# One hybrid pooling and attention layer on one core: unnormalised transposes, interleaved first tiles, tanh gates, and an output that is filled with x first and added to by DMA

## The reference

```
hn    = rmsnorm(concat(meta, x)) * norm_g              # 1040 x 2048
pv, pg, q, k, v, ag = split(hn @ w_in)                 # 1024,1024,1024,128,128,1024 columns
pool  = (trailing mean of pv over 2/4/8/16 frames - pv) @ pool_w[group] * pool_scale
attn  = softmax([q_n k_n^T / 8, sink]) v               # 16 q heads, 2 kv heads, head size 64;
                                                       # own and previous chunk of 64, meta always
mixed = concat(silu(pg) * pool, silu(ag) * attn)
out   = x + mixed @ w_out                              # meta rows dropped
```

## Time and profile before

| | |
|---|---|
| median of three executions | 1256.48 us |
| the profiled execution's own time | 1255.78 us |
| its span in the trace | 1254.1 us |
| PE busy | 1232.8 us (98%) |
| DVE busy | 896.8 us (72%) |
| ACT busy | 635.2 us (51%) |
| DMA | 134.38 MB, 107 GB/s over the span |

### The profile page before, as it was taken

One profiled execution on the slowest core, in us unless ns is written; L12 is line 12 of the kernel. 1 busy time (PEld: TensorE's weight loads), 2 busy tenths in 40 slices (PEclk: granted clock), 3 DMA queues, 4 the chain that ended last, 5 costly groups with the idle time before them and its releaser, 6 DMA issues.

```text
span 1254.1 us, 19307 instructions
## 1 busy us (share of the span) xinstructions
PE 1232.8 (98%) x6200; PEld 1041.8 (83%) x6200; DVE 896.8 (72%) x1425; ACT 635.2 (51%) x1490; POOL 67.8 (5%) x78
## 2 busy tenths in 40 slices
PE   4999999999999999999999999999999999999998
PEld 4988898898988978888888888888888888788887
DVE  7557786888879886565654677788798887854553
ACT  6434456465563655544533345655646557444442
POOL 0000000010020110000000000000101102000000
PEclk9999999999999999999999999999999999999999
DMA  5232333222332225544533332233322232333442
GB/s 217 80 93 78 97 95 85 84 73 71 102 89 76 79 67 201 185 134 160 192 120 91 92 102 85 85 84 86 99 76 85 76 99 86 116 127 128 165 142 84
DMA packets 70609, 134.38 MB, mean 107 GB/s; under 512 B 8064, under 2 KB 10240, under 8 KB 69888
## 3 DMA queue, kind: packets, MB, share of 16 engines
q1 hardware_dynamic: 68160, 125.17, 32.2%
q0 software_dynamic: 2384, 8.39, 1.9%
HBM read 125.14 MB, written 8.39 MB: 106 GB/s over the span
## 4 chain that ended last, share of the span: by engine, by line
PE 93%; DVE 3%; ACT 1%; DMA 1%; issue 1%; SPq 0%; DVEq 0%; ACTq 0%
PE R L1072 18%; PE R L1077 18%; PE R L1073 18%; PE S L1296 4%; PE S L1297 4%; PE S L1295 4%; PE OP L1297 2%; PE OP L1295 2%; PE R L1296 2%; PE OP L1296 2%; PE R L1297 2%; PE R L1295 2%; PE OP L1073 1%; PE OP L1072 1%; PE OP L1077 1%; PE S L1196 1%
## 5 line engine op out<-in xcount | busy, mean ns | idle before, releaser
L442 ACT ACTIVATE wh<-raw 128x512 fp32r<-128x512 f32 x400 | 250.3, 631 | 488.8 <-PE R L1077 265.0
L737 DVE TENSOR_TENSOR wl<-raw,wh 128x512 fp32r<-128x512 f32 x400 | 281.1, 706 | 237.1 <-ACT wh L442 235.9
L1072 PE MATMUL R<-act_h,wh 128*128 128x512 f32 (+1 forms) x1168 | 425.1, 369 | 0.2
L1073 PE MATMUL R<-act_l,wh 128*128 128x512 f32 (+1 forms) x1168 | 419.5, 364 | 0.0
L1077 PE MATMUL R<-act_h,wl 128*128 128x512 f32 (+1 forms) x1168 | 401.5, 364 | 0.0
L1072 PEld LDWEIGHTS R<-act_h,wh 128*128 128x128 f32 x1168 | 220.0, 188 | 34.8 <-DVE wl L737 0.9
L1073 PEld LDWEIGHTS R<-act_l,wh 128*128 128x128 f32 x1168 | 220.0, 188 | 32.7
L1077 PEld LDWEIGHTS R<-act_h,wl 128*128 128x128 f32 x1168 | 210.3, 188 | 35.8
L961 DVE RECIPROCAL scr<-scr 128x512 f32<-128x512 f32 x32 | 107.3, 3353 | 1.1
L414 POOL TENSOR_TENSOR scr<-scr 128x527 f32<-128x527 f32 (+3 forms) x40 | 49.8, 1245 | 793.0 <-ACT pv_last L442 363.3
L442 ACT ACTIVATE pm<-OP 16x128 fp32r<-16x128 f32 x256 | 68.3, 267 | 5.4
(11 more groups left out here) (206 smaller groups left out, 1825.7 us busy)
## 6 DMA issues: line engine op xcount, KB each, us to landing
raw<-w_in_blocks SPq DMA_DIRECT2D x272, 256.0 KB, 2.6
raw<-w_out_in SPq DMA_DIRECT2D x128, 256.0 KB, 3.0
scr<-xcat SPq DMA_DIRECT2D x32, 256.0 KB, 4.1
mixed<-xcat SPq DMA_DIRECT2D x4, 1024.0 KB, 7.6
res<-xcat SPq DMA_DIRECT2D x16, 256.0 KB, 3.2
out<-scr POOLq DMA_DIRECT2D x14, 256.0 KB, 2.6
out<-res POOLq DMA_DIRECT2D x14, 256.0 KB, 4.5
scr<-pool_w_in SPq DMA_DIRECT2D x8, 256.0 KB, 3.2
```

What stands on the lines that cost most here:

```text
L442: return nc.scalar.activation(dst, src, ACT.Copy)
L737: return nc.vector.tensor_tensor(dst, a, b, ALU.subtract)
L1072: mm(o, wh[:, b, w], xh, start=(k == 0), stop=False)
L1073: mm(o, wh[:, b, w], xl, start=False, stop=False)
```

## The change

- **No scaling before the transposes.** The raw frames of the first half are transposed, and only the gain norm_g is applied. The 528 reciprocal roots (and EPS times the mean square) are brought into rows `rb` and `r_eps` that hold a value for each frame on all partitions: ACT spreads them in `r_columns`, PE transposes them (`r_transposes`), ACT copies them out (`r_rows`). V, the gates and the pooled values of the first half are multiplied by `rb`; q and k, which are normalised anyway, only get `r_eps` in place of EPS (`k_mean`, `q_mean`).
- **First loads and first tiles.** The frames come in five loads by channel blocks (`FIRST_LOADS`: blocks 0-1, 2-3, 4-7, 8-11, 12-15), with the first weight blocks between them. The K and V tiles are interleaved block by block (`first_tiles`). `r_columns` stands on ACT ahead of Q slot 0, `r_transposes` on PE in Q slot 1, `r_rows` on ACT in slot 2, `q_mean(t)` on DVE in slot 4t + 5. The squares of K are summed in Q slot 2 and the V windows made in Q slot 8.
- **Gates by tanh.** silu(z) = z/2 (1 + tanh(z/2)): one activation and one DVE operation; in the first half one more DVE operation for `rb`. The factor 1/2 goes into `hscale` and the attention product.
- **Output.** After the last Q block of the first half SP issues eight copies from x to `out`, each 128 rows (1 MB), DRAM to DRAM. DVE only copies a product out of PSUM; POOL's queue adds it to `out` by an accumulating DMA. The residual loads and SP's last stores are gone.
- **Places.** The four operand buffers of the output projection that lie in `band_h` and `band_x` start at other columns; other tiles move with the size of `junk`, which is now part of `row_buf`.

```diff
-            sp.dma_start(x_meta, xcat[0:META, :]).then_inc(s_xf[ROWT], 16)
-            sp.dma_start(x_first[0], xcat[META:META + P, :]).then_inc(s_xf[0], 16)
-            sp.dma_start(cst[:, :], consts).then_inc(s_cst, 16)
...
+            def first_frames(i):
+                k0, k1 = FIRST_LOADS[i]
+                lo, hi = k0 % 4 * P, (k1 - 1) % 4 * P + P
+                sp.dma_start(mixed[:, k0 // 4:KT:4, lo:hi],
+                             xcat[META:META + HALF, k0 * P:k1 * P].rearrange("(r p) c -> p r c", p=P)).then_inc(s_xf[i], 16)
+            sp.dma_start(cst[:, 0:P], consts[:, 0:P]).then_inc(s_id, 16)
+            sp.dma_start(x_meta, xcat[0:META, :]).then_inc(s_xmeta, 16)
+            first_frames(0)
+            sp.dma_start(vec[:, :], vecs).then_inc(s_vec, 16)
+            first_block(0, free=False)
+            first_frames(1)
...
                 with sp.Fori(0, PAIRS) as j:
                     for b in range(TILE_BLKS):
                         n = KV_BLKS + j * TILE_BLKS + b
                         load_block(h0 + n, b % RAW, w_in[n, :, :])
+                if h == 0:
+                    for r in range(ROWT * HALVES):
+                        sp.dma_start(out[P * r:P * (r + 1), :], xcat[META + P * r:META + P * (r + 1), :]).then_inc(s_pre, 16)
                 sp.wait_ge(s_free, ONE + h * OB * ROWT)
...
-                        if RES_LOAD <= k < RES_LOAD + ROWT:
-                            r = k - RES_LOAD
-                            sp.dma_start(y[r], xcat[h * HALF + META + P * r:h * HALF + META + P * (r + 1),
-                                                    bass.ds(nb * BLK, BLK)]).then_inc(s_res[r], 16)
...
+                pool.wait_ge(s_pre, 16 * ROWT * HALVES)
+                with pool.Fori(0, OB) as nb:
                     for r in range(ROWT):
                         pool.wait_ge(s_ye, YB_FREE + (h * OB + nb) * ROWT + r + 1)
                         pool.dma_start(out[h * HALF + P * r:h * HALF + P * (r + 1), bass.ds(nb * BLK, BLK)],
-                                       y[r]).then_inc(s_out[r], 16)
+                                       y[r], accum_op=ALU.add).then_inc(s_out[r], 16)
...
+                        if h == 0:
+                            pool.tensor_tensor(pv_last[:, g * 2 + jj, :], pv[jj][:, COLS - META:COLS],
+                                               rb[:, COLS - META:COLS], ALU.mult).then_inc(s_pvl, 1)
+                            pool.tensor_tensor(pv[jj][:, :], pv[jj][:, :], rb[:, :], ALU.mult).then_inc(s_pvr, 1)
...
-        mix_h = [band_h[:, 0, 0:BLK], band_h[:, 1, 0:BLK],
+        mix_h = [band_h[:, 0, 64:64 + BLK], band_h[:, 1, 48:48 + BLK],
-        mix_l = [band_x[:, 0, 0:BLK], band_x[:, 1, 0:BLK], mix_x[:, 0, :], mix_x[:, 1, :]]
+        mix_l = [band_x[:, 0, 160:160 + BLK], band_x[:, 1, 144:144 + BLK], mix_x[:, 0, :], mix_x[:, 1, :]]
...
+                def r_columns():
+                    act.wait_ge(s_xrs, 2)
+                    for r in range(ROWT):
+                        copy(r_col[:, r, :], xrs[:, r:r + 1].to_broadcast([P, P])).then_inc(s_rc, 1)
+                        nc.scalar.activation(e_col[:, r, :], xsd[:, r:r + 1].to_broadcast([P, P]), ACT.Square,
+                                             scale=EPS ** 0.5).then_inc(s_rc, 1)
...
+                def r_rows():
+                    act.wait_ge(s_rt, 1)
+                    copy(rb[:, META:COLS], PT[:, :]).then_inc(s_rb, 1)
+                    copy(rb[:, 0:META], PM[:, 0:META]).then_inc(s_rb, 1)
+                    copy(r_eps[:, META:COLS], S[:, 1, :]).then_inc(s_rb, 1)
...
+                def q_mean(t):
+                    dve.wait_ge(s_qss, t + 1)
+                    nc.vector.scalar_tensor_tensor(q_rs[t % 2], (PT, PM)[t % 2][:, :], 1.0 / HD, r_eps[:, META:COLS],
+                                                   ALU.mult, ALU.add).then_inc(s_qm, 1)
...
-                        nc.vector.tensor_scalar(gate[n], gate[n], 1.0, None, ALU.add).then_inc(s_ga, 1)
-                        nc.vector.reciprocal(gate[n], gate[n]).then_inc(s_gr, 1)
-                        nc.vector.tensor_tensor(gate[n], bank[:, :], gate[n], ALU.mult).then_inc(s_gt[n], 1)
+                        tanh, u = (gate_t, gate[n]) if h == 0 else (gate[n], bank[:, :])
+                        nc.vector.scalar_tensor_tensor(gate[n], tanh, 1.0, u, ALU.add, ALU.mult).then_inc(s_gt[n], 1)
...
-                    nc.vector.tensor_tensor(y[r], YB[r], y[r], ALU.add).then_inc(s_ye, 1)
+                    nc.vector.tensor_scalar(y[r], YB[r], 1.0, None, ALU.mult).then_inc(s_ye, 1)
...
+            def first_tiles(h):
+                for n in range(KV_BLKS):
+                    b, banks = n // 2, (KB, VB)[n % 2][h]
+                    pe.wait_ge(s_wl, ONE + h * NBLK + n + 1)
...
                 def q_events(s):                       # PE, after each Q block
-                    if s == 0:
+                    if s == 1 and h == 0:
+                        r_transposes()
+                    elif s == 2:
+                        k_squares()
+                    elif s == 8:
                         v_windows()
```

More of the change, by code:

```diff
@@ L273, in hymba_layer @@
         s_ge = [sem(f"s_ge{n}") for n in range(4)]
-        s_ga = sem("s_ga")
-        s_gr = sem("s_gr")
+        s_gv = [sem(f"s_gv{n}") for n in range(4)]
         s_gt = [sem(f"s_gt{n}") for n in range(4)]
@@ L451, in split_high, with stats @@
                 copy(wh[:, slot, :], raw[:, slot, :]).then_inc(s_wh, 1)
-            def stats(x, rows, squares, n, col, loaded, loads):
-                act.wait_ge(loaded, 16 * loads)
+            def stats(x, rows, squares, n, col):
                 nc.scalar.activation(junk[0:rows, :], x[0:rows, :], ACT.Square,
@@ L494, in _ @@
                                      scale=vec[:, V_G + k:V_G + k + 1]).then_inc(s_xh, 1)
-                if k in FIRST_SPLITS and FIRST_SPLITS[k] >= RAW:
-                    split_high(0, FIRST_SPLITS[k])
+                for off in FIRST_SPLITS.get(k, ()):
+                    split_high(0, off)
+            act.wait_ge(s_cst, 16)
+            for i in range(len(FIRST_LOADS)):
+                act.wait_ge(s_xf[i], 16)
+            first_stats(0)
+            first_stats(1)
+            act.wait_ge(s_init, 5)
             for h in range(HALVES):
@@ L521, in _ @@
-                product_done(act, h, TILE_BLKS)
-                for bank, c in span_banks(h, VB[h]):
-                    own_v, frames = own_part(bank, c)
-                    copy(vT[:, CHUNK + frames.start:CHUNK + frames.stop], own_v).then_inc(s_vT, 1)
-                if h == 0:
-                    copy(v_meta[:, :], R[2][:, 0:META]).then_inc(s_vT, 1)
+                    if h == 0 and s < 7:
+                        first_stats(s - 3)
+                if h == 0:
+                    act.wait_ge(s_xm, 1)
+                    root(META, ROWT)
@@ L529, in v_all_out @@
+                if h == 0:
+                    r_columns()
                 def v_all_out():
@@ L703, in _ @@
                     group(g)
[L704 removed]
+                act.wait_ge(s_qn, (h + 1) * PAIRS)
                 group(2)
@@ new lines, in k_mean, with v_out @@
+                def k_mean():
+                    dve.wait_ge(s_rb, 4)
+                    dve.wait_ge(s_kss, 1)
+                    for bank, c in span_banks(h, (PT, PM)):
+                        nc.vector.scalar_tensor_tensor(k_rs[:, c], bank, 1.0 / HD, r_eps[:, c],
+                                                       ALU.mult, ALU.add).then_inc(s_km, 1)
+                def v_out():
+                    for bank, c in span_banks(h, VB[h]):
+                        own_v, frames = own_part(bank, c)
+                        nc.vector.tensor_tensor(vT[:, CHUNK + frames.start:CHUNK + frames.stop], own_v,
+                                                rb[:, META + frames.start:META + frames.stop],
+                                                ALU.mult).then_inc(s_vT, 1)
+                    nc.vector.tensor_tensor(v_meta[:, :], VB[h][0][:, 0:META], rb[:, 0:META],
+                                            ALU.mult).then_inc(s_vT, 1)
@@ L864, in _ @@
                         split_low(h4 + KV_BLKS // RAW, s + LEAD)
+                    if s == 1:
+                        k_square_low()
+                    if s == 3 and h == 0:
+                        k_mean()
+                        v_out()
+                    if s == 4:
+                        k_norm()
+                    if s > 4 and s % 4 == 1 and h == 0:
+                        q_mean(s // 4 - 1)
                     if s > 4 and s % 4 == 2:
@@ L1058, in _, with tile @@
             mm = nc.tensor.matmul
-            def tile(h, n, banks, cols, events=None, slot0=0, before=None, after=None):
+            def tile(h, n, banks, cols, events=None, slot0=0):
                 for b in range(TILE_BLKS):
@@ new lines, in r_transposes @@
+                def r_transposes():
+                    pe.wait_ge(s_rc, 2 * (ROWT + 1))
```

(15 more changed lines are left out.)

396 lines of the change are left out of this document (217 added, 179 removed).

## The result

The changed kernel takes 1275.22 us (median of 4 runs, 1274.03 to 1276.49). Beside it on the same chip the kernel before took 1256.62 us (1256.02 to 1257.13). The ratio is 1.0148, with a 95% interval of 1.0131 to 1.0166: slower by 18.6 us. The forecast was 1278.0 in a range of 1249 to 1289, with a chance of 0.71 for slower.

The account below looks back on a forecast made before the run. PE, busy 1232.8 of 1254.1 us, was taken as the bound. From 1255.8 us, -12.4 + 5.5 - 0.5 + 28.1 + 2.5 - 1.5 = +21.7 gave 1277.5, stated as 1278 us, range 1249 to 1289.

Parts of the forecast that it names:

- the copy: Copying x to out ahead of the first group's load in SP's queue stops PE: +28.1 us, second stop included.
- the tail: Kernel end: POOL issues the adding stores instead of SP's plain ones, +2.5 us, bounds 0.3 and 6.
- first product: Start of the kernel: PE's first product comes 12.4 us earlier, near 9.3 us, bounds 10 to 13.5.
- the row join: Q slots 1 and 2: PE waits 2 us in each for ACT, plus transposes and first Q norm; +5.5 us.
- gates and places, at the projections: Fewer DVE gate operations give 0.5 us; new operand columns in the output projections give 1.5, at most 2.6.
- The bound: Whole kernel: PE is nearly always busy, so work taken from DVE buys 1.4 us at most.
- so the first group's block lands after the copy: First group: its load stands behind the copy in SP's queue, landing with the split at 130.2 + P us.
- P: Duration of the copy of x to out, taken as 37 us, between 19 and 54; PE stops for P - 14.9.
- The second stop: Behind the first group's stop PE waits 5.4 us for DVE's low part and 0.6 more: 6.0, bounds 3 and 9.
- the copy runs at the loads' speed: Rival for the copy of x: P of 19 to 21 us, kernel time 1261 us; chance 0.17.
- the hidden case: Rival at the first group: its load doesn't stand behind the copy, or that lasts under 15 us; 1250 us, chance 0.22.
- a plain store landed after 4.5 us from POOL's queue and 2.3 from SP's: Kernel end: landing times of 256 KB stores, the basis for the output's +2.5 us with the adding store's read.

Follow-up runs that it names:

- experiment 10: Gates by Tanh and one operation instead of Exp, add, reciprocal and multiplication, as the one edit to the kernel before: 1254.15 us, ratio 0.9981.
- experiment 7: Changed kernel with the copies of x still in SP's queue at their place, but cut into 512 x 512 pieces: 1278.36 us, ratio 1.0168.
- experiments 5 and 6: Changed kernel with copies issued from GpSimd's queue at the same time: whole rows 1274.46 us, ratio 1.0146; cut into 512 x 512 pieces 1258.12 us, ratio 1.0009.
- experiment 8: Changed kernel with the old output method (1247.35 us), and the first half's gate_tanh(2) and gate_out(2) each one slot later: 1244.63 us, ratio 0.99.

## Why the prediction was right, and which of its terms were not

The direction, the place and the kind of the loss were right. The forecast was 2.8 us above the result, and that it came so near is luck: its terms were further off, and cancelled. The copy was taken 9.4 us too dear and the gain at the projections 3.3 too small; the tail and the groups, 6.5 and 3.7 us too cheap, made up for most of it. By PE's times in the two profiled executions (before to after):

| term | predicted | measured | from |
|---|---|---|---|
| first product | -12.4 | -11.1 | 21.74 to 10.68 |
| from there to slot 28, the row join in it | +5.5 | +4.2 | 136.23 to 129.35 is -6.9 |
| the copy | +28.1 | +18.7 | slot 0: 147.84 to 158.21, and the clock behind it |
| groups, first half | 0 | +3.7 | first projection: 465.09 to 480.55 is +15.5 |
| gates and places, at the projections | -0.5 and -1.5 | -5.3 | both shorter, by 2.6 and 2.7 |
| tail | +2.5 | +9.0 | 3.4 to 12.4 |

With -0.2 for the second half's groups that is +19.0; the spans differ by 18.9.

*The bound.* That PE's idleness was all there was to gain held well: 115 us of DVE brought 2.3 (experiment 10), within an interval that reaches down to 1.3. The bound given was 1.4, from idle times behind the recorded ends of products; from start to start the three waits that went are 1.65 us.

*The start.* The first product was 1.4 us later than worked out: the transposes of four channel blocks stand ahead of it on PE, not one group, and the second group of frames landed late (PE waits for it until 9.06). Another 1.2 us went behind it. Until 14.5 us a product of 128x264 follows the last after 0.22 us, afterwards after 0.12; before the change the slow pace ended at 23.2, after 6 products instead of 12. From the first product to the transposes behind the twelfth are 3.91 us, and were 2.67. (The view's PEclk reads 1.00 over this stretch, so what sets the pace is not shown.) So the first Q product gained 10.3 and not 12.9.
That the sum at slot 28 agreed to 0.1 us is in part luck. In slot 1 PE waits for ACT's columns, and these were done at 47.65, near the 47 of the forecast. PE came there at 46.97 instead of 44.6, so its own delay only shortened that wait, to 0.74. In slot 2 the rows were done at 51.91 instead of near 53, and the wait was 0.38 instead of 2. Which of ACT's operations was counted too long there was not taken apart.

*The copy.* The step "so the first group's block lands after the copy" was right, and its formula too. From SP's issue at 118.91, plus 1.95, plus P, plus 1.3, the block is there at 148.98, so P = 26.8 us; with that P the formula's stop, P - 14.9, is 11.9, and measured are 12.3. (P is worked back from the block's arrival; the copies' own times, from 118.9 + 1.95 to the last landing at 146.7, give 25.8.) The mis-sized term is P, taken as 37, and 26.8 also lies under the forecast's own 33 to 42. 8.39 MB in 26.8 us are 313 GB/s in each direction, near the loads' mean rate of 310 in the earlier trace rows; between 122 and 142 us, with the copies alone, it is 338. The instruction queue, taken as the nearest row, moves 35 packets in the whole span, and its share of 0.2% is rounded so coarsely that it allows 182 to 303 GB/s; its rate said little of a long stream. The Trainium skill's figure ("DMA: Bandwidth & Descriptors", "Latency and other measured facts", 207 to 214 GB/s) gave 40 us by my estimate. It is stated for tiles of 16 KiB rows that lie 512 KiB or more apart, and the copy here is contiguous; this trace shows 313 and does not bear the figure out for it.
The second stop, 5.4 us and 0.6 in the forecast, was one of 3.06. DVE's low part came 158.15 - 148.98 = 9.2 us after the block, forecast 9.6. But PE reached its slot later, since it ran at half clock for the first nine of twelve products. And the clock is a cost of its own that I left out: 12 products from 150.48 to 155.15 take 4.7 us instead of 2.8, and 8 from 158.21 to 161.56 take 3.35 instead of 1.86. Stop, second stop and the two costs of the clock are 12.3 + 3.1 + 1.9 + 1.5 = 18.8.
The rival "the copy runs at the loads' speed" (P = 19 to 21) was nearer in P than the forecast was. The reason given against the hidden case, the landings in line of the earlier trace rows, was true for one queue (experiment 7). It did not say what a second queue would do; experiments 5 and 6 show that there the packets decide.

*The groups.* The forecast had nothing here. The diff shows Tanh behind a new operation of DVE, in a list ahead of the value's parts. Each of three groups pays 0.5 to 0.6 us and the last 1.6, together 3.2; experiment 8 took 2.7 of it back. The other 0.5 of the 3.7 was not traced.

*The places.* Taken as 1.5 with 2.6 at the most; measured are 3.4 on PE in the changed kernel, and 2.4 to 2.6 as a difference of medians. The bound was too low: it took 2.74 of `v_s` as the floor, while all steps came down to 2.72.

*The tail.* Predicted 2.5 in bounds of 0.3 to 6, measured 9.0, outside them. The step that failed is "a plain store landed after 4.5 us from POOL's queue and 2.3 from SP's, and the adding one also has to read": it counted the queue's difference in landing (2.2) and almost nothing for the reading. The landing nearly doubled, and the issuer's own instructions came on top: four DMAs issued one behind another, the last two of them 2.20 us. The difference of the queues stood in the earlier trace rows, though only for the last two of the four stores; GpSimd's first two landed after 2.6 us in the same profile. Of the add there was no row, and the upper bound should have been a second landing (4.5) on top of the queue's difference, with the issues, some 9.

## What to carry to other kernels

A bulk transfer that nobody waits for can still have a price. Here whoever waited next in its queue paid all that was not hidden by loading ahead, and once it had a queue of its own, its packets decided how much the others got. Issue it in portions between the loads, or in small packets from another queue. Before a saving is counted, look for who stands idle: here 115 us of VectorE were worth 2.3 us, and a single operation ahead of the wrong one in ScalarE's list cost 2.7.

## What the runs showed of the hardware

- Two queues with work got turns by packet: 198 to 197 in 20 us. 99 of the 198 had 64 KB and held an engine for 3.1 us each, the 197 had 1 KB, so the second queue moved 0.20 MB of 6.69. Against copies in 4 KB packets it moved 1.79 MB in that time.
- The same pieces of 512 x 512 values, DRAM to DRAM, made packets of 2 KB in SP's queue and of 4 KB in GpSimd's.
- A copy from DRAM to DRAM ran at 313 GB/s in each direction over its whole length and 338 in its middle, in 64 KB packets, and at 303 in its middle in 2 KB packets (a stop of 16.0 us instead of 12.3).
- A store of 256 KB from GpSimd's queue landed after 4.9 us with the add and 2.7 without as one of the first two of four, and after 8.7 and 4.7 as one of the last two; from SP's queue after 2.3. Issuing two of the last took GpSimd 2.20 and 1.22 us.
- The columns at which TensorE's moving operands start in a buffer are worth up to 0.05 us in a step of 12 products (2.77 to 2.72). Why is open: the experiments moved four buffers at once, and no run tells which of them matters.
- After 12.3 us without work, and after 3.1 us so soon behind them, TensorE ran at the 1.2 GHz level for 3 to 4 us each.
